# The model dimension of a mixture-of-experts trunk split as block and partition

## The chip, the core and the metric

The program runs on one core of a Trainium2 chip. A core has TensorE (PE; PEld are its weight loads), VectorE (DVE), ScalarE (ACT), GpSimd (POOL) and SyncE (SP), which here only issues transfers, and 16 DMA engines. The metric is the device time of one execution in microseconds (us), the median of several runs. All data is float32, and a matrix product of float32 shows as two instructions in the trace.

## What is computed

Two decoder layers over 256 tokens of 1024 values, each a token mixer and then a mixture of 32 experts of which a token uses two. Shifts, scales and gates of every sub-layer come from one conditioning vector.

```python
c_act = silu(c)
for i in range(2):
    sh_m, sc_m, g_m, sh_f, sc_f, g_f = split(c_act @ ada_w[i] + ada_b[i], 6)
    h = rmsnorm(x, norm_mix_g[i]) * (1 + sc_m) + sh_m
    y = pool_mixer(h, ...) if i == 0 else moba_attention(h, w_qkv, w_o)
    x = x + g_m * y
    h = rmsnorm(x, norm_ffn_g[i]) * (1 + sc_f) + sh_f
    # top-1 group of 8 experts, then top-2 experts in it
    for e in range(32):
        he = silu(h @ w_gate[e]) * (h @ w_up[e])      # 1024 -> 256
        y2 = y2 + combine[:, e] * (he @ w_down[e])    # 256 -> 1024
    x = x + g_f * y2
return rmsnorm(x, final_norm_g)
```

## The kernel before

The weights, some 270 MB, are read once each and in the order of use. They pass through `ring`, four slots of 24 KB a partition (3 MB each). SyncE's program is one list of transfers in that order. Before each load it waits on `ring_free` of the slot, which the engine that reads the slot's contents last has raised; a reader waits on `ring_full`. A slot holds one expert (gate, up and down, 1 MB each), or one of the sixteen pieces of `ada_w` (`ada`, 768 columns), or a quarter of `w_qkv`, or half of `w_o`. `split3` (line 299 on) cuts the last three into transfers of three, three and two blocks; each transfer raises `ring_full` by 16, and the reader waits for 48.

To contract over the 1024 values of the model dimension, they are cut into 8 blocks (k) of 128 partitions (p). The kernel before takes d = p*8 + k in all weights that are contracted over it but those of w_o and pool_w. So a partition's part of one expert's gate matrix is eight rows that lie next to each other in memory, 8 KB in one run. The activations have to be cut in the same way: the block k of a token's row is every eighth value. That is the view `h_str` in `gather` (the product that gathers each expert's tokens and turns them), `xr` in `transposes`, and `src` in `col_piece`, all of them stationary operands of TensorE with a step of 8 values (32 bytes).

The order of the work: three pieces of ada, the pooling mixer with ada pieces 3 to 7 around it, the router (`route`), the gather, 32 experts in a loop; then ada pieces 8 to 10, attention with 11 to 15 in its gaps, the router, gather and 32 experts of layer 1, and the last norm. An expert e on TensorE (`expert`): the products with gate and up from its gathered tokens `xe` (32 instructions), the four transposes of the result of expert e-1 (`turn_last`), the transpose of `he`, and down (8 instructions). GpSimd copies the tokens of the next expert into `xe`, ScalarE makes the silu and stores the turned result, and VectorE makes `he` (silu times up, line 1217), copies `heT` and `ye`, and raises `ring_free` for the slot. The experts are sorted by slot range, and after experts 20, 24 and 28 (`STAGES`) a quarter of the results is turned back and combined into the tokens (`combine`, TensorE with line 630 and 8 products), if all of its tokens are in.

Nine of the sixteen pieces of ada are multiplied by TensorE (`part`), seven by VectorE (`ada_steps(a, k0, k1)`: the steps k0 to k1 of piece a, one instruction for a block k of 768 columns). VectorE's program has the steps of piece 8 inside layer 0's last experts: steps 0 to 2 behind expert 30, ahead of expert 31.

The shifts and scales of three sub-layers are needed as columns, a value to a partition (`col`), because the activations are turned there. Each such set of 16 columns comes from three pieces of ada: 4, 5, 6 before layer 0's router, 8, 9, 10 between the layers, 12, 13, 14 within the attention. `col_piece` turns each column with a product of its own: the piece `acc` is stationary and a vector of ones is the moving side. In the attention ScalarE then copies them out (`take_columns`). `columns` adds the bias `bcol` and the norm's weight `gcol`, which SyncE loads with six small transfers, as it loads the router's weights into `stage_g` and `stage_e`.

Of the kernel before, what the change touches and what calls it, by code (L numbers as in the profile page):

```python
# [14 lines left out]
P = 128  # L15
# [3 lines left out]
T = SEQ // P  # L19
# [43 lines left out]

COL_OF = {4: 0, 5: 1, 6: 2, 8: 0, 9: 1, 10: 2, 12: 0, 13: 1, 14: 2}
# [37 lines left out]

def program(nc, x, c, ada_w, ada_b, norm_mix_g, norm_ffn_g, pool_w, pool_scale, w_qkv, w_o,
            router_group_w, router_expert_w, exp_w_gate, exp_w_up, exp_w_down, final_norm_g, misc, band, out):
    ctx = ExitStack()
    with ctx:
# [34 lines left out]
        h_str = reg_h[:, :].rearrange("p (t q k) -> p t k q", t=T, k=KC)  # L141
        bcol = sb("bcol", [P, 2, 2, KC])
# [28 lines left out]
        gcol = sb("gcol", [P, 3, KC])  # L171
# [76 lines left out]
        gate_d = exp_w_gate.rearrange("l e (p k) f -> l e p (k f)", k=KC)  # L248
        up_d = exp_w_up.rearrange("l e (p k) f -> l e p (k f)", k=KC)
        down_d = exp_w_down.rearrange("l e (j p) d -> l e p j d", p=P)  # L250
        ada_d = ada_w.rearrange("l (p k) n -> l p k n", k=KC)
        qkv_d = w_qkv.rearrange("l (p k) (g n) -> l p k g n", k=KC, g=3)
        bias_d = ada_b.rearrange("l (v p k) -> l v p k", v=6, k=KC)
# [44 lines left out]
        def _(sp):  # L298
# [12 lines left out]
            def qkv(j):  # L311
                split3(QKV_AT[j], qkv_w(QKV_AT[j][0]), qkv_d[0, :, :, :, j * 256:j * 256 + 256])
# [4 lines left out]
            def expert(L, e, s, freed):  # L317
                sp.wait_ge(S("ring_free", s), freed)
                gsrc, usrc, dsrc = gate_d[L], up_d[L], down_d[L]
                sp.dma_start(ring[:, s, 0:2048], gsrc[bass.ds(e, 1), :, :].rearrange("a p n -> (a p) n"))\  # L320
                    .then_inc(S("ring_full", s), 16)
                sp.dma_start(ring[:, s, 2048:4096], usrc[bass.ds(e, 1), :, :].rearrange("a p n -> (a p) n"))\
# [93 lines left out]
        def _(pe):  # L416
# [51 lines left out]
            def col_piece(a, dst):  # L468

                pe.wait_ge(*acc_done(a))  # L470
                one = quarter[:, 0:1] if a in ADA_PE else ones[:, 0:1]

                def turned(lo, hi, p0, which):
                    src = acc[:, a % 2, lo:hi].rearrange("p (q k) -> p k q", k=KC)
                    n = (hi - lo) // KC
                    for k in range(KC):
                        at = which * KC + k
                        last = mm(dst[p0:p0 + n, at:at + 1], src[:, k, :], one, True, True)
                    return last
# [404 lines left out]
        def _(act):  # L884
# [114 lines left out]
            def overflow(L):  # L999
                act.wait_ge(S("dn_free", L), E + 2)  # L1000
                n_ovf = act.value_load(ov_i[0:1, L, 2 * MAXOVF:2 * MAXOVF + 1], min_val=0, max_val=MAXOVF)
                with act.If(n_ovf > 0):
                    with act.Fori(0, n_ovf) as i:
# [3 lines left out]
                        act.dma_start(reg_h[:, :], gate_d[L][bass.ds(e, 1), :, :].rearrange("a p n -> (a p) n"))\  # L1007
# [199 lines left out]
        def _(dve):  # L1207
# [61 lines left out]
            def columns(i, src):  # L1269

                if i == 0:
                    dve.wait_ge(S("gcol_loaded"), 32)
# [328 lines left out]
```

## Time and profile before

| | us |
|---|---|
| Median of 3 runs | 881.61 (878.8 to 884.11) |
| The profiled execution, its own time | 879.25 |
| Its span, from the first to the last instruction | 877.5 |

The profile of one execution, busy time over the span:

| Engine | busy us | share |
|---|---|---|
| PE | 750.7 | 86% |
| PEld | 439.3 | 50% |
| DVE | 255.6 | 29% |
| ACT | 173.8 | 20% |
| POOL | 42.2 | 5% |

The rows of the trace that follow further down come from these views. The page cuts the span into 40 slices of 21.9 us and prints a value for each. The timeline lists instructions in order of time; in brackets stands how long the engine was idle before, and what ended that. Neighbours of one form are merged into one row, whose length is from the first start to the last end. The table of windows gives, for each stretch, the busy time of each engine with its instructions, the granted clock of TensorE as a share of 2.4 GHz, the mean busy share of the DMA engines (it can be a little over 1), and what they moved in GB/s. Layer 0's experts run from about 134 to 374 us, layer 1's from about 620 to 859.

### The profile page before, as it was taken

How to read it: one execution, taken by the hardware profiler on the slowest of the kernel's cores; microseconds unless marked ns; L12 is line 12 of the kernel's file. 1: busy time of each engine (PE TensorE's matmuls, PEld its weight loads, DVE VectorE, ACT ScalarE, POOL GpSimd, SP SyncE). 2: the span in 40 equal slices, each digit the busy share in tenths (PEclk: the TensorE clock that was granted, in tenths of full speed). 3: DMA queues.
4: the chain of work that ended last, by engine and by line, in shares of the span. 5: the costliest groups of instructions: out<-in, count | busy, mean ns of one | idle time of the engine just before them, and what ended most of it. 6: DMA issues, size and time to landing. Idle time of an engine off the chain costs nothing.

```text
span 877.5 us, 12384 instructions
## 1 busy us (share of the span) xinstructions
PE 750.7 (86%) x4574; PEld 439.3 (50%) x4574; DVE 255.6 (29%) x648; ACT 173.8 (20%) x394; POOL 42.2 (5%) x73
## 2 busy tenths in 40 slices
PE   3699778999988998957999979966899999898994
PEld 1265544444444444435878756444444444444441
DVE  0050371121112112267448333048111111211114
ACT  1322322111111111124123222142211111101112
POOL 0010001000000000000000000000100100000000
PEclk9898679999999999976999979967999999999998
DMA  9999715999999999998386452170399999999931
GB/s 342 398 379 410 308 77 184 420 415 417 417 418 418 418 417 416 400 360 328 144 288 233 151 223 91 70 288 0 147 408 418 418 419 418 418 416 416 417 128 49
DMA packets 71578, 274.25 MB, mean 313 GB/s; under 512 B 5727, under 2 KB 19295, under 8 KB 55022
## 3 DMA queue, kind: packets, MB, share of 16 engines
q1 hardware_dynamic: 71534, 273.64, 78.8%
q8 instruction: 30, 0.49, 0.2%
q14 instruction: 14, 0.11, 0.0%
HBM read 272.57 MB, written 1.05 MB: 312 GB/s over the span
## 4 chain that ended last, share of the span: by engine, by line
PE 74%; DVE 7%; DMA 7%; ACT 5%; issue 3%; SPq 2%; ACTq 1%; DVEq 0%; POOLq 0%; POOL 0%
PE bank L418 70%; DMA ring<-in_exp_w_down_dram 5%; DMA ring<-in_ada_w_dram 2%; DVE reg_c L1217 2%; PE bank L557 2%; DVE heT L1414 2%; ACT reg_c L969 2%; SPq L305 1%; ACT reg_b L886 1%; PE bank L630 1%; ACT reg_b L936 1%; ACTq L983 1%; DVE ye L1217 1%; PE bank L769 1%; ACT reg_h L905 1%
## 5 line engine op out<-in xcount | busy, mean ns | idle before, releaser
L418 PE MATMUL bank<-ring,xe 128*64 128x256 f32 x2048 | 232.6, 380 | 5.1 <-POOL xe L393 3.1
L418 PEld LDWEIGHTS bank<-ring,xe 128*64 128x64 f32 x2048 | 148.0, 137 | 106.5 <-issue 37.9
L418 PE MATMUL bank<-ring,heT 128*64 128x512 f32 x512 | 124.0, 605 | 24.6 <-DVE heT L1414 20.3
L969 ACT ACTIVATE reg_c<-bank 128x128 f32<-128x128 f32 x64 | 17.7, 277 | 366.0 <-PE bank L418 366.0
L1217 DVE TENSOR_TENSOR reg_c<-reg_c,bank 128x128 f32<-128x128 f32 x64 | 18.4, 287 | 236.9 <-ACT reg_c L969 236.9
L1417 DVE COPY ye<-bank 128x512 f32<-128x512 f32 x64 | 44.3, 692 | 138.4 <-PE bank L418 138.4
L393 POOL COPY xe<-reg_a 128x512 f32 x64 | 39.3, 614 | 754.6 <-PE bank L418 410.8
L418 PEld LDWEIGHTS bank<-ring,heT 128*64 128x64 f32 x512 | 31.1, 136 | 73.3 <-DVE heT L1414 36.8
L418 PE MATMUL bank<-reg_b,ring 128*128 128x256 f32 x256 | 63.2, 405 | 0.0
L418 PEld LDWEIGHTS bank<-reg_b,ring 128*128 128x128 f32 x256 | 51.3, 204 | 11.0 <-issue 2.7
L886 ACT ACTIVATE reg_b<-bank 128x512 f32 (+1 forms) x72 | 41.5, 576 | 54.2 <-PE bank L570 36.7
L418 PE MATMUL bank<-ring,cact 128*32 128x512 f32 (+1 forms) x288 | 34.3, 606 | 20.0 <-DMA rows<-in_final_norm_g_dram 14.3
L1220 DVE SCALAR_TENSOR_TENSOR acc<-ring,cact,acc 128x768 f32<-128x768 f32 x49 | 49.8, 1016 | 1.4
L570 PE MATMUL bank<-cst,ye 128*128 128x128 f32 x256 | 42.0, 286 | 1.8 <-DVE ye L1417 1.8
L418 PE MATMUL bank<-reg_b,reg_h 128*128 128x512 f32 x64 | 32.7, 675 | 11.6 <-DVE reg_b L1220 11.6
L570 PEld LDWEIGHTS bank<-cst,ye 128*128 128x128 f32 x256 | 26.8, 141 | 27.4 <-issue 23.9
L418 PE MATMUL bank<-ring,reg_a 128*128 128x512 f32 (+1 forms) x96 | 35.5, 524 | 0.6 <-ACT reg_b L886 0.6
L557 PE MATMUL bank<-cst,reg_c 128*128 128x128 f32 x64 | 21.0, 328 | 13.1 <-DVE reg_c L1217 13.1
L418 PEld LDWEIGHTS bank<-reg_b,reg_h 128*128 128x128 f32 x64 | 20.1, 317 | 23.1 <-issue 12.6
L418 PE MATMUL bank<-ring,reg_b 128*128 128x256 f32 x128 | 29.9, 386 | 0.0
L1220 DVE SCALAR_TENSOR_TENSOR reg_c<-cst,bank 128x384 f32<-128x384 f32 x16 | 9.7, 608 | 59.1 <-PE bank L418 59.1
L418 PEld LDWEIGHTS bank<-ring,reg_b 128*128 128x128 f32 x128 | 23.8, 191 | 5.9 <-ACT reg_b L886 1.3
(138 smaller groups left out, 564.3 us busy)
## 6 DMA issues: line engine op xcount, KB each, us to landing
ring<-in_exp_w_gate_dram SPq DMA_DIRECT2D x64, 1024.0 KB, 12.2
ring<-in_exp_w_up_dram SPq DMA_DIRECT2D x64, 1024.0 KB, 14.3
ring<-in_exp_w_down_dram SPq DMA_DIRECT2D x64, 1024.0 KB, 16.3
ring<-in_ada_w_dram SPq DMA_DIRECT2D x32, 1152.0 KB, 10.0
ring<-in_ada_w_dram SPq DMA_DIRECT2D x16, 768.0 KB, 12.7
ring<-in_w_qkv_dram SPq DMA_DIRECT2D x8, 1152.0 KB, 9.7
ring<-in_w_qkv_dram SPq DMA_DIRECT2D x4, 768.0 KB, 11.7
ring<-in_w_o_dram SPq DMA_DIRECT2D x4, 768.0 KB, 7.6
```

The source lines that it names most:

```text
L305: sp.dma_start(dst[:, a:b], src[:, a:b]).then_inc(S("ring_full", s), 16)
L393: nc.gpsimd.tensor_copy(xe[:, b, :, :], hS[:, :, bass.ds(off, CAP)]).then_inc(S("xe_ready", L), 1)
L418: return nc.tensor.matmul(o_, l_, r_, start=start, stop=stop)
L557: return nc.tensor.transpose(dst[:, 2 * P:3 * P], he[:, b, :], ident)
L570: last = nc.tensor.transpose(dst[:, cq * P:(cq + 1) * P], ye[:, b, cq * P:(cq + 1) * P], ident)
L630: last = nc.tensor.transpose(bank[half][:, mq * P:(mq + 1) * P], yT[:, half * 4 + mq, s * P:(s + 1) * P], ident)
L886: return nc.scalar.activation(o_, i_, ACT.Identity)
L969: nc.scalar.activation(sil[:, b, :], bank[b][:, 0:P], ACT.Silu).then_inc(S("sil_ready", L), 1)
L1217: return nc.vector.tensor_tensor(o_, a_, b_, op)
L1220: return nc.vector.scalar_tensor_tensor(o_, a_, s_, b_, op0, op1)
L1414: nc.vector.tensor_copy(heT[:, b, :], bank[b][:, 2 * P:3 * P]).then_inc(S("heT_ready", L), 1)
L1417: nc.vector.tensor_copy(ye[:, b, :], bank[2 + b][:, :]).then_inc(S("ye_ready", L), 1)
```

## The change

All weights contracted over the model dimension are read as d = k*128 + p, except `ada_w` and `c`. A gate or up matrix then goes to a partition in eight runs of 1 KB, 128 KB apart in memory. `h_str`, `xr` and `src` become blocks of 128 values side by side. `w_qkv` is fetched in three transfers by q, k and v in place of three by blocks; its runs are of 1 KB before and after. The router's weights come in runs of 16 bytes (group) and 128 bytes (expert), before of 128 bytes and 1 KB. `col_piece` turns 6, 6 and 4 blocks of 128 columns (16 products a set) in place of 8, 16 and 8 strided ones of 32 to 96 columns (32 products). Bias and norm weights of the columns are put in order on the host and come in one transfer `vecs`, which takes the place of six.

```diff
+COL_AT = (((8, 14),), ((14, 16), (0, 4)), ((4, 8),))
+COL_0, COL_N = (0, 6, 12), (6, 6, 4)
...
-        h_str = reg_h[:, :].rearrange("p (t q k) -> p t k q", t=T, k=KC)
-        bcol = sb("bcol", [P, 2, 2, KC])
+        h_str = reg_h[:, :].rearrange("p (t k q) -> p t k q", t=T, k=KC)
...
-        gate_d = exp_w_gate.rearrange("l e (p k) f -> l e p (k f)", k=KC)
-        up_d = exp_w_up.rearrange("l e (p k) f -> l e p (k f)", k=KC)
+        gate_d = exp_w_gate.rearrange("l e (k p) f -> l e p k f", k=KC)
+        up_d = exp_w_up.rearrange("l e (k p) f -> l e p k f", k=KC)
...
-        qkv_d = w_qkv.rearrange("l (p k) (g n) -> l p k g n", k=KC, g=3)
+        qkv_d = w_qkv.rearrange("l (k p) (g n) -> l p k g n", k=KC, g=3)
...
             def qkv(j):
-                split3(QKV_AT[j], qkv_w(QKV_AT[j][0]), qkv_d[0, :, :, :, j * 256:j * 256 + 256])
+                s, turn = QKV_AT[j]
+                sp.wait_ge(S("ring_free", s), turn)
+                for g in range(3):
+                    sp.dma_start(qkv_w(s)[:, :, g, :], qkv_d[0, :, :, g, j * 256:j * 256 + 256])\
+                        .then_inc(S("ring_full", s), 16)
...
-                sp.dma_start(ring[:, s, 0:2048], gsrc[bass.ds(e, 1), :, :].rearrange("a p n -> (a p) n"))\
+                sp.dma_start(gate_w(s), gsrc[bass.ds(e, 1), :, :, :].rearrange("a p k f -> (a p) k f"))\
...
-            sp.dma_start(gcol[:, 0:2, :], norm_ffn_g.rearrange("l (p k) -> p l k", k=KC)).then_inc(S("gcol_loaded"), 16)
-            sp.dma_start(gcol[:, 2, :], norm_mix_g[1].rearrange("(p k) -> p k", k=KC)).then_inc(S("gcol_loaded"), 16)
-            sp.dma_start(stage_g, router_group_w.rearrange("l (p k) n -> p l k n", k=KC)).then_inc(S("stage_loaded"), 16)
-            sp.dma_start(stage_e, router_expert_w.rearrange("l (p k) n -> p l k n", k=KC)).then_inc(S("stage_loaded"), 16)
-            for i, v0 in enumerate((0, 3)):
-                for which in range(2):
-                    sp.dma_start(bcol[:, i, which, :], bias_d[1, v0 + 1 - which]).then_inc(S("bcol_loaded"), 16)
+            sp.dma_start(vec[:, :], vecs).then_inc(S("vecs_loaded"), 16)
+            sp.dma_start(stage_g, router_group_w.rearrange("l (k p) n -> p l k n", k=KC)).then_inc(S("stage_loaded"), 16)
+            sp.dma_start(stage_e, router_expert_w.rearrange("l (k p) n -> p l k n", k=KC)).then_inc(S("stage_loaded"), 16)
...
-                if COL_OF[a] == 0:
-                    return turned(0, AC, 0, 1)
-                if COL_OF[a] == 1:
-                    turned(0, 256, 96, 1)
-                    return turned(256, AC, 0, 0)
-                return turned(0, 512, 64, 0)
+                for j in range(COL_N[COL_OF[a]]):
+                    at = (COL_0[COL_OF[a]] + j + KC) % (2 * KC)
+                    last = mm(dst[:, at:at + 1], acc[:, a % 2, j * P:(j + 1) * P], one, True, True)
+                return last
...
-                xr = h_of[i].rearrange("p t (q k) -> p t k q", k=KC)
+                xr = h_of[i].rearrange("p t (k q) -> p t k q", k=KC)
...
-                    dve.wait_ge(S("bcol_loaded"), 64)
                     then(tt(col[:, i, :, :], src, bcol[:, i - 1, :, :], ALU.add))
```

## Rows read from the trace of the kernel before

**Rows 1.** The page's line of what the DMA engines moved, 40 slices
```profile
GB/s 342 398 379 410 308 77 184 420 415 417 417 418 418 418 417 416 400 360 328 144 288 233 151 223 91 70 288 0 147 408 418 418 419 418 418 416 416 417 128 49
```
**Rows 2.** The page, the chain that ended last, shares of the span by line
```profile
PE bank L418 70%; DMA ring<-in_exp_w_down_dram 5%; DMA ring<-in_ada_w_dram 2%; DVE reg_c L1217 2%; PE bank L557 2%; DVE heT L1414 2%; ACT reg_c L969 2%; SPq L305 1%; ACT reg_b L886 1%; PE bank L630 1%; ACT reg_b L936 1%; ACTq L983 1%; DVE ye L1217 1%; PE bank L769 1%; ACT reg_h L905 1%
```
**Rows 3.** Timeline of PE, layer 0, two experts' gate and up: start us, us, engine line
```profile
175.11 3.62 PE L418 MATMUL bank<-ring,xe 128*64 128x256 f32 x32
...
181.98 3.62 PE L418 MATMUL bank<-ring,xe 128*64 128x256 f32 x32
```
**Rows 4.** Timeline of PE, layer 0, gate and up of experts 16, 20 and 31
```profile
244.05 3.67 PE L418 MATMUL bank<-ring,xe 128*64 128x256 f32 x32
...
274.37 3.67 PE L418 MATMUL bank<-ring,xe 128*64 128x256 f32 x32 [0.63 <-DMA ring<-in_exp_w_down_dram]
...
367.29 3.62 PE L418 MATMUL bank<-ring,xe 128*64 128x256 f32 x32
```
**Rows 5.** Timeline of PE, layer 1, gate and up of experts 20, 21 and 31
```profile
759.16 3.67 PE L418 MATMUL bank<-ring,xe 128*64 128x256 f32 x32
...
771.75 3.67 PE L418 MATMUL bank<-ring,xe 128*64 128x256 f32 x32
...
852.32 3.62 PE L418 MATMUL bank<-ring,xe 128*64 128x256 f32 x32
```
**Rows 6.** Timeline of PE, layer 1, a combine's eight unstrided products, 512 wide
```profile
768.15 3.67 PE L418 MATMUL bank<-mod,reg_c 128*128 128x512 f32 x8 [0.88 <-DVE mod L1440]
```
**Rows 7.** Windows while pool_w, w_qkv, w_o, ada_w and experts load, in this order
```profile
42.00:44.00 2.00, 2.00 (x8) 0.53 (x11) 0.95 (x2) 0.00 (x0) 0.00 (x0) 1.00 1.10 348
...
482.00:486.00 4.00, 4.00 (x23) 3.56 (x22) 0.00 (x0) 0.78 (x3) 0.00 (x0) 1.00 1.09 351
488.00:490.00 2.00, 2.00 (x13) 1.56 (x12) 0.00 (x0) 0.38 (x1) 0.00 (x0) 1.00 1.05 389
50.00:58.00 8.00, 8.00 (x34) 6.01 (x33) 0.37 (x1) 2.39 (x4) 0.00 (x0) 1.00 1.03 404
166.00:196.00 30.00, 27.35 (x193) 14.20 (x194) 5.36 (x13) 4.01 (x9) 2.84 (x5) 1.00 1.02 416
```
**Rows 8.** Timeline of DVE behind expert 30 of layer 0: piece 8, then expert 31's product
```profile
368.24 0.61 DVE L1238 TENSOR_SCALAR acc<-ring,cact 128x768 f32<-128x768 f32 x1
368.89 2.07 DVE L1220 SCALAR_TENSOR_TENSOR acc<-ring,cact,acc 128x768 f32<-128x768 f32 x2
371.34 0.29 DVE L1217 TENSOR_TENSOR reg_c<-reg_c,bank 128x128 f32<-128x128 f32 x1 [0.38 <-ACT reg_c L969]
```
**Rows 9.** Windows at the end of layer 0's experts (columns as in Rows 7)
```profile
376.00:380.00 4.00, 0.00 (x0) 0.00 (x0) 3.18 (x4) 0.60 (x1) 0.00 (x0) 0.97 1.04 388
380.00:384.00 4.00, 0.88 (x4) 0.88 (x5) 0.00 (x0) 0.00 (x0) 0.00 (x0) 0.50 1.09 349
```
**Rows 10.** Timeline of PE: column pieces 4, 5 with 6, 12, 13, 14; unstrided short products
```profile
75.72 3.04 PE L418 MATMUL bank<-cst,acc 128*96 128x1 f32 x16
...
83.72 4.62 PE L418 MATMUL bank<-cst,acc 128*32 128x1 f32 x48
...
106.21 0.53 PE L418 MATMUL bank<-ye,ones 128*128 128x32 f32 x4
...
107.02 0.39 PE L418 MATMUL bank<-ye,cst 128*128 128x32 f32 x2
...
453.57 2.93 PE L418 MATMUL bank<-ones,acc 128*96 128x1 f32 x16
...
473.91 3.15 PE L418 MATMUL bank<-ones,acc 128*32 128x1 f32 x32
...
489.21 2.08 PE L418 MATMUL bank<-ones,acc 128*64 128x1 f32 x16
```
**Rows 11.** Timelines of PE and PEld: eight transposes, then layer 1's gather weight loads
```profile
71.19 1.16 PE L503 MATMUL bank<-cst,reg_h 128*128 128x128 f32 x8 [0.80 <-ACT reg_h L905]
...
605.07 11.47 PEld L418 LDWEIGHTS bank<-reg_b,reg_h 128*128 128x128 f32 x27 [0.49 <-issue]
```

More of the change, by code:

```diff
@@ L100, in constants, with by_columns @@
     return {"misc": np.ascontiguousarray(misc), "band": band}
+def by_columns(ada_b, norm_mix_g, norm_ffn_g):
+    b = np.asarray(ada_b).reshape(2, 6, D)
+    rows = [norm_ffn_g[0], norm_ffn_g[1], norm_mix_g[1], b[1, 1], b[1, 0], b[1, 4], b[1, 3]]
+    return np.stack([np.asarray(r) for r in rows]).reshape(7, KC, P).transpose(2, 0, 1).reshape(P, 7 * KC)
 def program(nc, x, c, ada_w, ada_b, norm_mix_g, norm_ffn_g, pool_w, pool_scale, w_qkv, w_o,
-            router_group_w, router_expert_w, exp_w_gate, exp_w_up, exp_w_down, final_norm_g, misc, band, out):
+            router_group_w, router_expert_w, exp_w_gate, exp_w_up, exp_w_down, final_norm_g, vecs, misc, band, out):
     ctx = ExitStack()
@@ L170, in program @@
         spare = sb("spare", [P, 1])
-        gcol = sb("gcol", [P, 3, KC])
+        vec = sb("vec", [P, 7 * KC])
+        gcol = vec[:, 0:3 * KC].rearrange("p (i k) -> p i k", i=3)
+        bcol = vec[:, 3 * KC:7 * KC].rearrange("p (i w k) -> p i w k", i=2, w=2)
         col = sb("col", [P, 3, 2, KC])
@@ L319, in expert @@
                 gsrc, usrc, dsrc = gate_d[L], up_d[L], down_d[L]
-                sp.dma_start(ring[:, s, 0:2048], gsrc[bass.ds(e, 1), :, :].rearrange("a p n -> (a p) n"))\
+                sp.dma_start(gate_w(s), gsrc[bass.ds(e, 1), :, :, :].rearrange("a p k f -> (a p) k f"))\
                     .then_inc(S("ring_full", s), 16)
-                sp.dma_start(ring[:, s, 2048:4096], usrc[bass.ds(e, 1), :, :].rearrange("a p n -> (a p) n"))\
+                sp.dma_start(up_w(s), usrc[bass.ds(e, 1), :, :, :].rearrange("a p k f -> (a p) k f"))\
                     .then_inc(S("ring_full", s), 16)
@@ L471, in col_piece @@
                 one = quarter[:, 0:1] if a in ADA_PE else ones[:, 0:1]
[L473 to L479, printed above, removed]
-                if COL_OF[a] == 0:
-                    return turned(0, AC, 0, 1)
-                if COL_OF[a] == 1:
-                    turned(0, 256, 96, 1)
-                    return turned(256, AC, 0, 0)
-                return turned(0, 512, 64, 0)
+                for j in range(COL_N[COL_OF[a]]):
+                    at = (COL_0[COL_OF[a]] + j + KC) % (2 * KC)
+                    last = mm(dst[:, at:at + 1], acc[:, a % 2, j * P:(j + 1) * P], one, True, True)
+                return last
             def ada(a):
@@ L1103, in take_columns @@
             def take_columns(name, a):
-                src = unit(name)[:, 0:2 * KC].rearrange("p (w k) -> p w k", w=2)
-                if COL_OF[a] == 0:
-                    copy(craw[0:96, 1, :], src[0:96, 1, :]).then_inc(S("unit_read"), 1)
-                elif COL_OF[a] == 1:
-                    copy(craw[96:128, 1, :], src[96:128, 1, :])
-                    copy(craw[0:64, 0, :], src[0:64, 0, :]).then_inc(S("unit_read"), 1)
-                else:
-                    copy(craw[64:128, 0, :], src[64:128, 0, :]).then_inc(S("unit_read"), 1)
+                craw_f = craw[:, :, :].rearrange("p w k -> p (w k)")
+                src = unit(name)
+                for lo, hi in COL_AT[COL_OF[a]]:
+                    last = copy(craw_f[:, lo:hi], src[:, lo:hi])
+                last.then_inc(S("unit_read"), 1)
             def exps(m):
@@ L1271, in columns @@
                 if i == 0:
-                    dve.wait_ge(S("gcol_loaded"), 32)
+                    dve.wait_ge(S("vecs_loaded"), 16)
                 if i < 2:
@@ L1592 @@
     arrays, args = {}, {}
-    for name, a in [(n, inputs[n]) for n in _INS] + list(constants().items()):
+    vecs = by_columns(inputs["ada_b"], inputs["norm_mix_g"], inputs["norm_ffn_g"])
+    for name, a in [(n, inputs[n]) for n in _INS] + [("vecs", vecs)] + list(constants().items()):
         a = _np.ascontiguousarray(a)
```

7 lines of the change are left out of this document (4 added, 3 removed).

## The prediction

> **What bounds the kernel now.** I read the page's slices first: the transfer rate stands at 415 to 418 GB/s through most of layer 0's experts and again through layer 1's [rows 1]. The chain of what ended last gives TensorE's products 70% and the transfer of the expert's last matrix only 5% [rows 2]. The two do not contradict each other, and the timeline of TensorE shows why. One expert's gate and up matmuls start 6.87 us after those of the expert before (175.11 to 181.98) [rows 3]: that is TensorE's own pace. One expert's weights are 3 x 1.0486 MB, and at 416 to 418 GB/s they take over 7.5 us: the transfers are the slower of the two. The ring holds four experts, so TensorE starts each layer with a lead and loses it at 0.7 us per expert. In layer 0 it is used up at expert 16 (244.05); experts 16 to 20 start every (274.37 - 244.05) / 4 = 7.58 us, which I take as the period of the transfers [rows 4]. In layer 1 the lead ends at expert 20 (759.16) [rows 5]. The three combines in the last twelve experts then give TensorE extra work (771.75 - 759.16 = 12.59 us from one expert to the next, 5.7 more than 6.87), and the transfers get ahead again. So the loop is balanced to about 0.7 us per expert, and any slower transfer comes straight through.
>
> **Part 1, the expert weights in 1 KB runs.** Before, a gate or up matrix goes to a partition in one run of 8 KB; after, in eight of 1 KB. The trace of before holds 1 KB runs too, in w_qkv and pool_w, each in a stretch of its own, so their rate can be read alone. In the windows of the bulk transfers [rows 7] pool_w (1 KB rows that lie side by side in memory, as the new gate matrix's will) moves at 348 GB/s, w_qkv (1 KB rows far apart) at 351, w_o (2 KB) at 389, ada_w (3 KB) at 404, the experts' mix of 8 and 4 KB at 416. The share of the DMA engines is full in all five, so this is the rate of the run length and not a lack of work. I take 351, from the longer of the two 1 KB windows; 348 is the other end. One matrix then takes 1.0486 / 351 = 2.99 us in place of 1.0486 / 416 = 2.52, or 0.47 more; two of them 0.94; the period becomes 7.58 + 0.94 = 8.52 us (8.58 at 348 GB/s). With layer 0's first expert at 244.05 - 16 x 6.87 = 134.1 and layer 1's at 759.16 - 20 x 6.87 = 621.8, the lead is gone by the ninth expert in the one and the eleventh in the other.
>
> The Trainium skill (DMA: Bandwidth & Descriptors, Why small descriptors are slow) gives a packet a fixed 3 cycles beside one for each 32 bytes. By it a 1 KB run costs 35 cycles for 32, some 8% over an 8 KB run, and by that alone the period would be 8.0; the 348 and 351 GB/s of [rows 7] are 16% below 416, twice as much. Its Specifications table asks only 512 B for line rate, by which the change would cost nothing here; [rows 7] speak against that too.
>
> Layer 0: TensorE's expert 16 started when its weights had landed, so expert 4, the first loaded inside the loop, landed at 244.05 - 12 x 7.58 = 153.1. After: expert n lands at 153.1 + 0.94 + 8.52 (n - 4), so 28 at 358.5 and 31 at 384.1. Expert 28's combine lets 31 start at 358.5 + 12.59 + 2 x 6.87 = 384.8, against 367.29 now [rows 4].
>
> The wait behind it: VectorE's program has the first three steps of ada piece 8 between experts 30 and 31, now at 368.24 to 370.96, and expert 31's product only after them, at 371.34 [rows 8]. SyncE issues piece 8 behind expert 31, and with the queue full it lands 3.146 MB / 404 GB/s = 7.8 us after it, at 391.9. VectorE stands on that wait with expert 31's product queued behind, and TensorE, ScalarE and the tail wait for the product. It starts at 391.9 + 2.7 = 394.6, 23.2 us later than now; without this hold it would be 17.5. TensorE idles some 6 us for it. A like idle stretch now takes its clock from 0.97 to 0.50, the 1.2 GHz level [rows 9], so expert 31's down product (1.94 us) and what follows would run at half speed: +2.0 (0 to 4).
>
> Layer 1: 759.16 - 16 x 7.58 = 637.9 for expert 4; after, 28 lands at 637.9 + 0.94 + 24 x 8.52 = 843.3 and 31 starts at 843.3 + 12.59 + 13.74 = 869.6 against 852.32 [rows 5]: +17.3. Nothing but the tail follows.
>
> **Part 2, columns by whole blocks.** Each set of shift and scale columns took 64 TensorE instructions (32 products, two instructions each) with a stationary operand strided by 8; it takes 32 after, 128 wide and without stride. A contiguous load of 128 with a short product goes every (107.02 + 0.39 - 106.21) / 10 = 0.12 us, ten instructions in all [rows 10]. Before layer 0's router, 3.04 + 4.62 us [rows 10] become 12 x 0.12 + 20 x 0.12 to 0.24 (half clock is possible): a gain of 1.4 to 3.8, I take 2.8. In the attention, where TensorE is busy without a gap, 2.93 + 3.15 + 2.08 [rows 10] become 32 x 0.12 = 3.8; the gain is up to 4.3, and ScalarE's reads of the same banks may take some back: 3.8 (1 to 4.3). Between the layers piece 8's product is hidden, as TensorE then waits for piece 9 on VectorE; 0.3.
>
> **Part 3, gathers and transposes without stride.** The gather's weight loads are the longest of the kernel, but 27 of them start within 11.47 us, one per 0.425 us [rows 11], while the combine's eight products, as wide and without a stride, last 3.67 us, 0.46 each with their tail [rows 6]. The moving side paces both: no gain (0 to 1). Eight strided transposes take 1.16 us [rows 11]; a few hundredths each at most: 0.3 in all.
>
> **Part 4, small loads.** Six vector loads become one; the router weights come in 4096 runs of 16 and 128 B in place of 512 of 128 B and 1 KB. They may hold ada pieces 4 to 7 back by 1 to 3 us. Cover: those pieces are wanted from 65 us on, and the first experts not before 133. With it gone, up to 3. The wait for bcol goes; nothing was late on it. w_qkv keeps its 1 KB runs and only the grouping changes: 0.
>
> **The sum.** 23.2 + 2.0 + 17.3 - 2.8 - 3.8 - 0.3 - 0.3 = +35.3. On the profiled execution's 879.25 that is 914.6; the median shown, 881.61, is 2.4 above it and would give 916.9. I say 915. The bounds: rate +3.3, hold -5.7, clock -2 to +2, gains -2 to +4.5, small loads +3: 903 to 927. I widen it to 898 to 930, since the rate of 1 KB runs is read from windows of 2 and 4 us and must hold for 450.
>
> **Rivals.**
> - Half the price (7 in 100): next to each other in memory and with nothing mixed in, the new runs move like w_o's 2 KB rows, 389 GB/s. One matrix costs 2.70, the period is 7.94; both layers lose the 0.36 x 17 = 6.1 us up to expert 20, after which the combines give TensorE the lead back; the hold costs 1. 879.25 + 13.2 - 7.2 = 885. For it: the rate rises with the run. Against: pool_w lies side by side too, and gave 348. The 3-cycle rule of the Trainium skill, above, would land near here.
> - Faster (4 in 100): the new runs keep the full rate and parts 2 and 3 are left alone: 879.25 - 7.2 = 872. The point where it tips: 2 x 17 experts x the rise of the period = 7.2, a rise of 0.21, or a matrix in 2.62 us: 400 GB/s. 1 KB rows would have to beat the 3 KB rows' neighbourhood.
> - The clock (7 in 100): TensorE now waits 8.52 - 6.87 = 1.65 us in each of some 45 experts. If that lets its clock fall to the lower level in every third, that expert's 6.5 us of products double, of which 3.3 are won back in the next two: 15 x 3.2 = 48 at worst, about half that where the clock returns within the expert: 915 + 24 = 939. For it: [rows 9]. Against: there the idle stretch was over 7 us, and between 244 and 274 the waits of half a microsecond left the pace alone.
> - Otherwise 2 in 100; the forecast 80 in 100.
>
> **Chances.** A measurement of this kernel tells about 0.5% (4.4 us) from no change. Faster 0.04, the same 0.01, slower 0.95.
>
> **What would show it.** Rate in the expert stretches near 370 GB/s with the engines' share full (3.146 / 8.52 = 369); 128 matrices x 128 partitions x 7 = 115 thousand more packets; experts 8.5 us apart from the ninth on in layer 0 and the eleventh in layer 1, TensorE's waits put down to the weights' transfers; VectorE held before expert 31 of layer 0 by ada_w; column products halved in number and shorter; the gather as long as before. It would be wrong if the rate stays above 400, if the experts keep 6.87, or if the clock row drops inside the loops.

## The result and the profile after

The kernel after takes 907.95 us (median of 4 runs, 907.04 to 908.52) against 882.86 for the kernel before: ratio 1.029, 95% interval 1.024 to 1.034. That is slower by 25.1 us; the forecast was 915. The profiled execution has a span of 905.7 us against 877.5. The page of the kernel after, what the DMA engines moved and the chain of what ended last:

```profile
GB/s 346 381 357 384 366 21 346 369 365 367 369 363 367 367 364 369 378 388 373 226 279 272 100 232 139 103 176 1 331 368 363 369 368 363 369 365 365 369 266 47
...
PE 42%; SPq 40%; DVE 7%; DMA 5%; issue 3%; ACT 3%; POOLq 0%; DVEq 0%; POOL 0%; ACTq 0%
PE bank L427 39%; SPq L337 18%; SPq L335 16%; DMA ring<-in_ada_w_dram 4%; SPq L333 3%; SPq L314 2%; DVE acc L1218 2%; DMA ring<-in_exp_w_down_dram 1%; DVE reg_c L1215 1%; PE bank L556 1%; DVE x_sb L1215 1%; DVE heT L1411 1%; ACT reg_c L968 1%; PE bank L629 1%; DVE ye L1215 1%
```

Where 415 to 418 GB/s stood [rows 1], 363 to 369 stand in both layers' experts, and where TensorE's products were 70% of the chain [rows 2], SyncE's queue (SPq, the issues of gate, up and down) now has 40%. The DMA engines are full (windows of the kernel after, layer 0's and layer 1's experts; columns as in [rows 7], the last three are granted clock, share of the DMA engines, GB/s):

```profile
200.00:380.00 180.00, 148.87 (x993) 78.69 (x991) 28.09 (x65) 20.23 (x45) 12.28 (x20) 1.00 1.07 367
...
700.00:850.00 150.00, 122.38 (x822) 63.72 (x818) 23.55 (x55) 16.99 (x38) 11.02 (x18) 1.00 1.07 367
```

A rival is that SyncE itself is too slow, as it now issues 1024 runs for a matrix. Its timeline speaks against it (gate and up early in layer 0, then up and down in the transfer-bound stretch):

```profile
142.20 0.37 SPq L333 DMA_DIRECT2D ring<-in_exp_w_gate_dram  x1
142.66 0.53 SPq L335 DMA_DIRECT2D ring<-in_exp_w_up_dram  x1
...
251.74 4.57 SPq L335 DMA_DIRECT2D ring<-in_exp_w_up_dram  x1
256.40 3.40 SPq L337 DMA_DIRECT2D ring<-in_exp_w_down_dram  x1
```

The same 1024 runs are issued in half a microsecond early on and stand for 4.57 us later; down, whose runs did not change, stands for 3.40 us there and for 0.8 to 1.4 in the kernel before. So the issues are held up by what is in front of them, and SyncE's 40% of the chain are the transfers' time.

The timeline of TensorE of the kernel after: gate and up of layer 0's experts 8, 9 and 10; what lies behind expert 31; and the column pieces that answer to [rows 10].

```profile
183.01 3.62 PE L427 MATMUL bank<-ring,xe 128*64 128x256 f32 x32
...
191.04 3.67 PE L427 MATMUL bank<-ring,xe 128*64 128x256 f32 x32 [0.98 <-issue]
...
199.63 3.67 PE L427 MATMUL bank<-ring,xe 128*64 128x256 f32 x32 [1.51 <-issue]
...
380.41 3.62 PE L427 MATMUL bank<-ring,xe 128*64 128x256 f32 x32
...
390.43 0.47 PE L556 MATMUL bank<-cst,reg_c 128*128 128x128 f32 x1 [5.81 <-DVE reg_c L1215]
391.28 3.33 PE L427 MATMUL bank<-ring,heT 128*64 128x512 f32 x8 [0.38 <-DVE heT L1411]
...
397.37 1.85 PE L629 MATMUL bank<-cst,reg_b 128*128 128x128 f32 x8 [1.18 <-ACT reg_b L885]
```

```profile
76.22 1.50 PE L427 MATMUL bank<-cst,acc 128*128 128x1 f32 x12
...
81.09 2.39 PE L427 MATMUL bank<-cst,acc 128*128 128x1 f32 x20
...
467.62 1.40 PE L427 MATMUL bank<-ones,acc 128*128 128x1 f32 x12
```

Seen there: the ninth expert after the first is the first to wait; the period is (276.83 - 191.04) / 10 = 8.58 us. TensorE then stands 5.81 us ahead of expert 31's turned product. The column pieces take half of what they did.

Two rows of the kernel before were not among those of the prediction, and bear on it. The first is the unstrided ada product behind the first column set; the second answers to the last row of the first fence (timeline of TensorE of the kernel before, transposes of layer 0's last combine):

```profile
78.69 3.02 PE L418 MATMUL bank<-ring,cact 128*32 128x512 f32 x16
...
383.12 1.97 PE L630 MATMUL bank<-cst,reg_b 128*128 128x128 f32 x8 [7.21 <-issue]
```

In the second, TensorE waits 7.21 us for nothing that the profile shows; after, 1.18. The difference of the two timelines, step by step (us; each is a start in after minus the same start in before, less the steps above it):

| step | forecast | measured |
|---|---|---|
| to layer 0's expert 0 (133.84 to 128.01) | -3.1 | -5.8 |
| experts 0 to 31 (367.29 to 380.41, less the line above) | +17.5 | +19.0 |
| expert 31 to VectorE's product for it (371.34 to 390.09) | +5.7 | +5.6 |
| its down product at half clock, to the last turn | +2.0 | +1.5 |
| the unnamed wait ahead of the last combine | 0 | -6.0 |
| between the layers (412.01 to 425.76 at the q product) | -0.3 | -0.5 |
| attention (512.43 to 520.15) | -3.8 | -6.0 |
| to layer 1's expert 0 (619.51 to 627.11) | 0 | -0.1 |
| layer 1's experts (852.32 to 879.26) | +17.3 | +19.3 |
| the tail | 0 | +1.3 |
| sum (the terms are rounded) | +35.3 | +28.2 |

### The profile page after: what moved, and what is told of

It is laid out like the page before. It is cut to its first block, busy times and chain, and to the rows that moved or that the text cites. A ratio compares the mean times of both kernels' runs of the same rounds, so it can differ in the third digit from the quotient of the medians.

```text
span 905.7 us, 12185 instructions
## 1 busy us (share of the span) xinstructions
PE 744.1 (82%) x4478; PEld 425.1 (47%) x4478; DVE 255.8 (28%) x648; ACT 173.4 (19%) x394; POOL 40.5 (4%) x73
## 2 busy tenths in 40 slices
DMA packets 189001, 274.23 MB, mean 303 GB/s; under 512 B 8719, under 2 KB 153103, under 8 KB 188830
## 4 chain that ended last, share of the span: by engine, by line
PE 42%; SPq 40%; DVE 7%; DMA 5%; issue 3%; ACT 3%; POOLq 0%; DVEq 0%; POOL 0%; ACTq 0%
PE bank L427 39%; SPq L337 18%; SPq L335 16%; DMA ring<-in_ada_w_dram 4%; SPq L333 3%; SPq L314 2%; DVE acc L1218 2%; DMA ring<-in_exp_w_down_dram 1%; DVE reg_c L1215 1%; PE bank L556 1%; DVE x_sb L1215 1%; DVE heT L1411 1%; ACT reg_c L968 1%; PE bank L629 1%; DVE ye L1215 1%
## 5 line engine op out<-in xcount | busy, mean ns | idle before, releaser
L427 PEld LDWEIGHTS bank<-ring,xe 128*64 128x64 f32 x2048 | 150.4, 137 | 142.9 <-issue 51.0
L427 PEld LDWEIGHTS bank<-reg_b,reg_h 128*128 128x128 f32 x64 | 13.7, 217 | 28.9 <-issue 24.0
L1411 DVE COPY heT<-bank 128x128 f32<-128x128 f32 x64 | 18.7, 292 | 27.0 <-PE bank L556 27.0
```

The costliest lines, as they stand in the source:

```text
L427: return nc.tensor.matmul(o_, l_, r_, start=start, stop=stop)
L1411: nc.vector.tensor_copy(heT[:, b, :], bank[b][:, 2 * P:3 * P]).then_inc(S("heT_ready", L), 1)
```

## The experiments

Four questions: is it the length of a run that costs, and on which side; is the hold worth what it was priced at; what made the columns faster than forecast; and where did 6 us ahead of the last combine go. Times are medians; ratios are against the kernel before in the same session.

### The run length

**runs8, runs4, runs2**: the kernel after, with gate and up in runs of 8, 4 and 2 KB (the first line of the edit; the writes into the ring follow it). The experts' values are then not those of the reference; the amount of work is the same.

```diff
-        gate_d = exp_w_gate.rearrange("l e (k p) f -> l e p k f", k=KC)
+        gate_d = exp_w_gate.rearrange("l e (a p b) f -> l e p a (b f)", p=P, b=RUN)
```

> The kernel after, with gate and up matrices fetched in one run of 8 KB a partition as before; their rows then do not match the tokens' blocks, so the experts' values are other ones. Theory (the whole loss is the length of the runs, and all else in the change is gain): transfers back at 416 GB/s, experts paced by them 7.58 us apart and only from expert 16 on, no TensorE wait of 6 us before expert 31's product; the gains seen in after stay (5.8 us before layer 0's experts, 6.6 between the layers): about 865 us of span, 0.985 of before. Rival (the small loads, the grouping of w_qkv or the block layout itself cost something that the slow transfers cover): 870 us or more of span.

> The kernel after, with the gate and up matrices fetched in runs of 4 KB (d = a*512 + p*4 + b); everything else as after, so the gate and up products take other rows of h than the reference wants. Theory (rate follows the run length): down has had 4 KB runs all along; at 404 to 416 GB/s a matrix takes 2.52 to 2.60 us, the period is 7.56 to 7.72, and TensorE's lead lasts to expert 16 or further in both layers: 861 to 866, I say 862. If the cost is the number of pieces on the chip's side alone, 8 KB and 4 KB would be alike too: 861. Over 870 would say that the 8 KB run is worth more than its neighbours show.

> The kernel after, with the gate and up matrices fetched in runs of 2 KB (d = a*256 + p*2 + b) in place of 1 KB; everything else as after, so the gate and up products take other rows of h than the reference wants. Theory (the rate follows the run length; after's period of 8.58 us per expert leaves 8.58 - 2.52 = 6.06 us for two matrices, 346 GB/s): at the 389 GB/s that w_o's 2 KB runs had, a matrix takes 2.70 us, the period is 2.52 + 2 x 2.70 = 7.92 us. Layer 0's expert 31 starts about 27 x 0.66 = 18 us earlier than after's 380.4, but no earlier than TensorE's own pace allows (360.4 in runs8): 362 to 366; the same in layer 1. Time 873, range 866 to 880. Rival (the number of runs per issue, not their size, costs SyncE its time; 512 runs per matrix in place of 1024): the excess over 8 KB would be halved too, so it gives about the same here and isn't told apart by this run. Rival (only runs under 2 KB cost): 861.

Measured: 860.87 us (ratio 0.975, 0.970 to 0.980) with 8 KB, 864.76 (0.980, 0.973 to 0.987) with 4 KB, 876.7 (0.9955, 0.992 to 0.999) with 2 KB, against 907.95 with 1 KB. Windows inside layer 0's transfer-bound stretch, of the kernel with 4 KB and of the kernel with 2 KB:

```profile
243.00:267.00 24.00, 19.98 (x138) 10.83 (x140) 4.23 (x11) 3.23 (x7) 2.46 (x4) 1.00 1.03 410
```

```profile
200.00:272.00 72.00, 59.44 (x412) 31.57 (x410) 11.98 (x29) 8.75 (x20) 6.10 (x10) 1.00 1.04 394
```

The periods are 7.58 us at 8 KB (the kernel before, [rows 4], and runs8, (267.51 - 244.77) / 3), 7.68 at 4 KB ((266.93 - 243.89) / 3 in the timeline), 7.98 at 2 KB ((272.10 - 224.25) / 6) and 8.58 at 1 KB. The excess over 8 KB is 0.10, 0.40 and 1.00 us for 256, 768 and 1792 more runs per expert: it grows with their number, and on 16 engines is by our estimate 6 to 9 ns for each run. The whole loss of this change is in that factor: with 8 KB runs what is left of the change makes the kernel 2.5% faster. runs2 and runs4 lie in the ranges expected for them; runs8 has a span of 857.6 us, 7 under the 865 expected, as the expectation did not count that the 6.0 us ahead of the last combine are gone here too. So some 6 of its gain of 21 us belong to that wait (below).

**before_1k**: the kernel before, its 8 KB runs of memory kept, but each spread over the ring in 1 KB pieces (up likewise; TensorE's view of the slot follows).

```diff
-                sp.dma_start(ring[:, s, 0:2048], gsrc[bass.ds(e, 1), :, :].rearrange("a p n -> (a p) n"))\
+                both = ring[:, s, 0:4096].rearrange("p (k g f) -> p k g f", k=KC, g=2)
+                sp.dma_start(both[:, :, 0, :], gsrc[bass.ds(e, 1), :, :].rearrange("a p (k f) -> (a p) k f", k=KC))\
```

> The kernel before, with gate and up interleaved block by block in the ring, so that each of their transfers lands in eight pieces of 1 KB while the source stays one run of 8 KB a partition; nothing else changes. Theory (a transfer moves in pieces of 1 KB as soon as one side has them, and that alone costs): 367 GB/s and 8.58 us an expert as in after, time 881 + 19 + 19 + 1 = about 920 us, 1.045 of before. Rival (the cost comes from where the rows lie in memory, 128 KB apart): 416 GB/s, 7.58 us, time as before within 3 us.

Measured: 923.93 us (1.044, 1.038 to 1.050); window of layer 0's experts:

```profile
200.00:380.00 180.00, 147.55 (x975) 77.67 (x973) 28.27 (x66) 20.23 (x45) 12.94 (x21) 1.00 1.07 366
```

366 GB/s, as in the kernel after, though memory is read in the old order. In the kernel after it is the other way round: 1 KB rows in memory, 8 KB side by side in a partition of the ring. So it is not where the rows lie in memory: the smaller run of the two sides counts. By itself this part costs the kernel before 42 us, more than the 25 of the whole change.

### The hold

**no_hold**: the kernel after, VectorE's first three steps of ada piece 8 moved behind expert 31.

```diff
-                        if L == 0 and e + u == E - 2:
-                            ada_steps(8, 0, 3)
...
-                    ada_steps(8, 3, 7)
+                    ada_steps(8, 0, 7)
```

> The kernel after, with the first three steps of ada piece 8 moved from ahead of expert 31's product to behind it on VectorE. Theory A (the hold hides another wait: in before TensorE stood 6.5 us ahead of the last combine with nothing that the profile shows, in after it stood 6 us ahead of expert 31's transpose and then only 1.2 there): expert 31's product comes 6 us earlier, the wait ahead of the combine grows back to 7 us, and the time stays within 2 us of after's 908. Rival B (the hold costs what the prediction said, 5.7 us or more): about 902 us.

Measured: 903.24 us (1.023, 1.019 to 1.027), 4.7 under after. Timeline of TensorE, the last combine of layer 0:

```profile
389.31 1.15 PE L629 MATMUL bank<-cst,reg_b 128*128 128x128 f32 x8 [1.18 <-ACT reg_b L885]
...
395.01 5.46 PE L427 MATMUL bank<-reg_h,reg_c 128*128 128x512 f32 x6 [4.55 <-DVE reg_h L1437]
```

The transposes start 8.06 us earlier than in after (397.37), the product behind them only 5.30 (400.31): VectorE now has all seven steps of piece 8 ahead of the copy of reg_h, and TensorE waits 4.55 us for that. The time is that of rival B (about 902), so the hold and its price are shown; a step moved out of one queue position was again late at the next.

### Stride or number

**apart**: the kernel before, with ada pieces stored so that TensorE reads its columns without a stride (all but piece 14); still 32 products per set, 8 KB runs.

```diff
+            return acc[:, a % 2, 0:n].rearrange("p (k q) -> p k q", k=KC)
...
+                if split:
+                    dst = apart(a)
+                def block(k):
+                    return w[:, k, :].rearrange("p (q c) -> p c q", c=KC) if split else w[:, k, :]
```

> The kernel before, with 8 KB runs and the same 32 column products a set; only the pieces of ada that become columns are stored with the eight values of a partition apart, so that the stationary operands have no stride (all but piece 14). Theory (the stride is what makes the column products slow, some 1.9 ns a column): the sixteen 96-wide ones go from 2.9-3.0 us to about 1.8, the others a little shorter, TensorE's clock stays up behind them; 3 to 6 us less than before, 876 to 879 us. Rival (the number of products decides, stride or not): within 1.5 us of before.

**col_stride**: the kernel after, its products 128 wide and 16 to a set, but strided by 6 values; the columns then hold other values than the reference wants.

```diff
+                src = acc[:, a % 2, :].rearrange("p (q j) -> p j q", j=6)
-                    last = mm(dst[:, at:at + 1], acc[:, a % 2, j * P:(j + 1) * P], one, True, True)
+                    last = mm(dst[:, at:at + 1], src[:, j, :], one, True, True)
```

> The kernel after with its 16 column products per set kept in number (128 wide), but each stationary operand strided by 6 values in place of contiguous, so the columns hold other values than the reference wants. It tells the stride apart from the number of products: after's sets last 1.50 and 2.39 us before layer 0's router and 1.40, 1.40, 0.95 in the attention, before's 3.04, 4.62 and 2.93, 3.15, 2.08 with twice the number, 96 wide and strided by 8. Theory (the stride is what costs, as the kernel with de-interleaved pieces had 32 contiguous products in 1.52 and 2.59 us): the sets take 2 us or more where 1.50 stood and 3 or more where 2.39 stood, and the attention's 2 us or more where 1.40 stood; the whole kernel 3 to 8 us slower than after: 912. Rival (the number of products costs): no change, 908, the sets 1.50, 2.39, 1.40, 1.40, 0.95 as before. Also expected by the first: the granted clock in the windows behind the sets (80 to 85 us and 500 to 505 us) falls back from 0.85 and 1.00 to about 0.7 and 0.6, as in the kernel before.

Measured: apart takes 873.15 us (0.989, 0.985 to 0.993), 3 us under the expected range, and is faster than both kernels. Timeline of TensorE, its sets before layer 0's router, to be laid beside the 3.04 and 4.62 of [rows 10]:

```profile
75.94 1.52 PE L423 MATMUL bank<-cst,acc 128*96 128x1 f32 x16
77.39 1.92 PE L423 MATMUL bank<-ring,cact 128*32 128x512 f32 x16
...
80.83 2.59 PE L423 MATMUL bank<-cst,acc 128*32 128x1 f32 x48
```

And of the kernel col_stride, with half as many:

```profile
76.31 2.83 PE L427 MATMUL bank<-cst,acc 128*128 128x1 f32 x12
79.06 2.80 PE L427 MATMUL bank<-ring,cact 128*32 128x512 f32 x16
...
84.09 4.60 PE L427 MATMUL bank<-cst,acc 128*128 128x1 f32 x20
```

Nearly all of the gain is the stride's: without it, the full number of products is about as fast as half of them (1.52 and 2.59 against 1.50 and 2.39); with it, half of them take as long as the full number. The second line of each fence shows what was missed in the forecast: the ada product behind the set has no stride in any kernel and takes 2.80 us behind a strided set (3.02 in the kernel before) and 1.92 behind an unstrided one. The granted clock, third from the end, tells why (windows 79 to 82 us, just behind the first set, of before, col_stride, after and apart):

```profile
79.00:82.00 3.00, 3.00 (x24) 0.55 (x16) 0.00 (x0) 0.00 (x0) 0.00 (x0) 0.56 1.02 423
...
79.00:82.00 3.00, 3.00 (x21) 0.71 (x25) 0.00 (x0) 0.00 (x0) 0.00 (x0) 0.66 1.06 370
...
79.00:82.00 3.00, 3.00 (x48) 1.62 (x41) 0.00 (x0) 0.98 (x2) 0.00 (x0) 1.00 1.06 366
...
79.00:82.00 3.00, 3.00 (x62) 1.87 (x58) 0.00 (x0) 0.98 (x2) 0.00 (x0) 1.00 1.02 424
```

Behind the strided set the clock spends most of these 3 us at the 1.2 GHz level (0.50), and what follows pays; behind the unstrided one it does not. Further on the stride makes no such difference: between 88 and 90 us, behind the second set, the granted clock is 0.50 in all four. Layer 0's first expert starts at 134.34 us in col_stride, 133.84 in before, 128.01 in after and 127.64 in apart. The time of col_stride as a whole, 971.89 us (1.103, 1.095 to 1.110), can't be used: with other column values the router fills its experts otherwise and the overflow part runs (2352 packets of a second queue that no other run has). So of its expectation only the sets and the clock are tested, not the 912 us.

**gather_stride**: the kernel after, with the stationary operands of transposes and gathers strided by 8 values; h is then taken in another order than the weights want.

```diff
-        h_str = reg_h[:, :].rearrange("p (t k q) -> p t k q", t=T, k=KC)
+        h_str = reg_h[:, :].rearrange("p (t q k) -> p t k q", t=T, k=KC)
```

> The kernel after with the stationary operands of the transposes and of the gather strided by 8 values again, all else contiguous as after, so h is taken in another order than the weights want. Theory (the moving side paces the gather): the gathers last as long as after's 16.67 and 15.67 us within 0.3, the eight transposes 1.16 in place of 1.10, the whole within 1 us of after's: 908. Rival (the strided load paces where the clock is full): each gather 1 us longer or more, 910 or above. The mean of a weight load should rise from 217 to about 317 ns in both.

Measured: 907.59 us (1.028, 1.021 to 1.036), as after. Weight loads by form (count, busy us, mean ns), of after and of gather_stride:

```profile
L427 PEld LDWEIGHTS bank<-reg_b,reg_h 128*128 128x128 f32 x64 | 13.7, 217 | 28.9 <-issue 24.0 <-DVE reg_b L1218 4.8
```

```profile
L427 PEld LDWEIGHTS bank<-reg_b,reg_h 128*128 128x128 f32 x64 | 20.1, 317 | 22.5 <-issue 11.9 <-DVE reg_b L1218 4.8
```

A load takes 100 ns longer with the stride, and it costs nothing, as it lies beside a 512-wide product; layer 0's gather takes 16.56 us against 16.67.

### The wait ahead of the last combine

The kernels with the code of after had no such wait (after, no_hold, gather_stride and the three with longer runs), those with the code of before had it (before 7.21 us, apart 7.17, before_1k 6.93), with and without a hold. What sets the two groups apart is, among other things, where TensorE's instructions lie. At this place TensorE jumps over the overflow part. Its instructions come in packets of 16 KB. Taking 256 to a packet, as the section of the Trainium skill named below does, the jump goes in before from its instruction 3304 to about 3590, which is from block 12 into block 14; in after from 3240 to 3526, block 12 into 13. These numbers are an estimate from the program, no row of the trace shows them, and 3590 lies only 6 behind the start of block 14. The trace has this: in the kernel before, the DMA rows show one packet of instructions between 380 and 382 us, inside the wait, and none in the 25 us ahead of it. Two kernels move the code and nothing else, before_shift with the lines below in the kernel before, after_shift with 64 in place of 32 in the kernel after:

```diff
+            for _ in range(32):
+                pe.sem_inc(S("shift"), 1)
             for a in range(3):
                 ada(a)
```

> The kernel before with 32 increments of a semaphore that nobody reads ahead of TensorE's first product (it waits there for the first transfer anyway), so that all of TensorE's later instructions stand 32 places further on; nothing else. Instructions take 64 bytes and the trace fetches them in packets of 16 KB, so 256 to a block. At the end of layer 0 TensorE jumps over the overflow part: in the kernel before from instruction 3304 to about 3590, from block 12 into block 14; here from 3336 to 3622, from block 13 into block 14; in the kernel after from 3240 to 3526, block 12 into 13; in layer 1 always into the next block. Theory (the 7.2 us of issue wait ahead of the last combine of layer 0 is the fetch of a block that is not the next one): it goes, the transposes start about 1.2 us after ScalarE's copy, at 377 in place of 383.1. VectorE's products for ada piece 9 are next in line before the attention; they start as much earlier, so most of it reaches the end: 877 (875 to 880). Rival (the wait belongs to the semaphores or to the DMA's load at that place, which are the same here): the gap stays 7.2, 882.5.

> The kernel after with 64 such increments ahead of TensorE's first product, which puts the jump over layer 0's overflow part where it stands in the kernel before (from instruction 3304, block 12, into block 14). Theory of the code fetch: the wait of some 7 us comes back ahead of the transposes of the last combine of layer 0, which started at 397.37 with 1.18 of wait in after and would start at 403 to 404; VectorE's and TensorE's later work goes with it: 913 (910 to 915). Rival (that the hold on ada piece 8 takes the wait's place, or that it belongs to the transfers): as after, 908.

Measured: before_shift 872.01 us (0.990, 0.988 to 0.993), 3 under its expected range; after_shift 908.36 (1.033, 1.029 to 1.036), where 913 was expected and the rival said 908. The transposes, in before_shift:

```profile
378.23 1.97 PE L630 MATMUL bank<-cst,reg_b 128*128 128x128 f32 x8 [1.28 <-ACT reg_b L888]
```

and in after_shift, with the DMA rows of its window 394 to 396 us:

```profile
396.87 1.97 PE L629 MATMUL bank<-cst,reg_b 128*128 128x128 f32 x8 [1.96 <-issue]
```

```profile
q8 instruction: 1, 0.02, 3.5%
```

32 increments that nobody reads take the wait away and make the kernel before 1% faster; its span falls by 5.4 us. In before_shift a packet of instructions comes at 372.6 us, ahead of the jump, and none in the gap between turn and transposes. A second pair says the same: apart_part (below) waits 7.07 us, with a packet inside, and with the 32 increments (apart_shift) 1.29. That the wait is for a block of code fetched on demand is shown by these two pairs.

How long such a fetch takes is not shown, and here the expectation of after_shift failed: the packet comes right behind the jump, and the wait grows by 0.8 us, where the four kernels with the full wait lose some 6. In before the packet starts 5.3 us after expert 31's turn does (375.25 to 380.53), in after_shift 0.1 us after it (394.25 to 394.32). It is not the hold that covers it (before_1k has a hold of 5.85 us and the full wait). In those four, w_qkv was issued as 768 and 1152 KB transfers by then, in after_shift as 1024 KB ones; whether the fetch queues behind them was not tried. Nor is it shown why the median fell by 9.7 us where the span of the profiled execution fell by 5.4; the runs of before spread from 876.7 to 887.6 in that session, those of before_shift from 871.4 to 873.8, and the profiled execution of before_shift is the slowest of its six.

The Trainium skill (Runtime: NRT & Kernel Launch, Instruction fetch mechanics) says that fetching is sequential, in blocks of 256 instructions, and that a taken branch out of what is loaded has to fetch its target before it goes on. The trace agrees in that the packet falls into the wait; for the length of the wait no run here gives a rule.

### A better version

**apart_part** leaves pieces 8 and 9, which VectorE makes between the layers, as they were; **apart_shift** adds the 32 increments to it.

```diff
-                    if a == 14:
+                    if a in (8, 9, 14):
...
-                split = a in COL_OF and COL_OF[a] < 2
+                split = a in (12, 13)
```

> The kernel with de-interleaved ada pieces, but pieces 8 and 9, which VectorE makes between the layers, left as in the kernel before (VectorE writes them without a stride, TensorE reads them with one); pieces 4, 5, 6 and 10 (copied by ScalarE) and 12, 13 (VectorE, in the attention) stay de-interleaved. Theory: between the layers VectorE is the one waited for (7.33 us at 400.24 in the kernel with all of them, its six steps there 1.62 us each against 1.02), so the path to the attention gets 3.6 us back and loses about 1 on piece 9's products: 870.6 for the span becomes 868, the time 870.5 (868 to 873). If the strided steps of VectorE were hidden: 874 or more.

> The same as the kernel that leaves pieces 8 and 9 alone, plus the 32 increments ahead of TensorE's first product (jump at the end of layer 0 from instruction 3336 to 3622, block 13 into 14). Theory: both gains add, as they lie one behind the other: 870.5 - 5.5 = 865 (862 to 868), which would be the fastest correct kernel of this case, 2% under before. If VectorE's work between the layers doesn't start earlier with it, 870.

Measured: apart_part 874.83 us (0.993, 0.991 to 0.996): the expectation of 870.5 was wrong. The attention's q product does start 2.96 us earlier than in apart (407.61 against 410.57), as expected, but of this 1.66 us are left 80 us later, and 9 us further on apart_part is 0.7 behind. Timeline of TensorE behind piece 14's strided set, in apart and in apart_part:

```profile
487.16 0.87 PE L423 MATMUL bank<-ye,reg_b 128*64 128x256 f32 x8
487.96 0.93 PE L423 MATMUL bank<-reg_a 64*128 64x128 f32 x8
```

```profile
485.50 1.55 PE L423 MATMUL bank<-ye,reg_b 128*64 128x256 f32 x8
486.98 1.65 PE L423 MATMUL bank<-reg_a 64*128 64x128 f32 x8
```

The same program text there, the same strided set ahead, and the granted clock between 484 and 488 us is 1.00 in apart and 0.50 in apart_part. The eight products take 1.55 us in before, before_shift and apart_shift too, and 0.87 in before_1k; what decides it is not shown. apart_shift, with the wait gone as well, takes 868.30 us (865.32 to 871.25; 0.986, 0.983 to 0.989). That is at the upper end of what was expected (865, 862 to 868). It keeps the 8 KB runs, and is 13 us under before and some 40 under after; 10 of the 13 come with the increments alone (before_shift). apart with the increments, the next thing to try, was not run.

## Why the prediction was right, and where it was not

- **The rate.** Right in kind, a little off in size: period 8.52 forecast from w_qkv's 351 GB/s, 8.58 measured, which is what pool_w's 348 had given [rows 7]. Over both layers that makes +38.3 in place of 34.8. A few microseconds of a transfer read alone foretold 450 us of it to 1%.
- **The lead.** First waits at expert 9 of layer 0 and expert 10 of layer 1, ninth and eleventh forecast. The working took expert 31's landing as a fixed time, while the sum took the columns' gain off it as well. The runs bear the sum out: the loads start when TensorE frees their slots, so an earlier first expert makes them all earlier. By the sum expert 31 would start 14.4 us later than before, and it does 13.1. Layer 1's first expert, put at 621.8, stands at 619.51 in before: 2.0 us of other products lie behind expert 3, in both kernels, so this costs the forecast nothing.
- **The hold and the clock behind it.** 5.7 forecast, 5.6 in the trace, 4.7 by no_hold; half clock +2.0 forecast, +1.5 measured.
- **Columns.** The step that was mis-sized: 2.8 and 3.8 us forecast, 5.8 (with 0.3 of the transposes) and 6.0 measured. The sets alone gained 3.8 (7.66 to 3.89) and 4.4 (8.16 to 3.75), the upper ends of their ranges. The working priced the products alone and took the rows around them as they were; the 3.02 us product behind the set in before was itself slowed by it. The half-clock rows behind the sets were in the trace to be read.
- **Gathers, transposes, small loads.** No gain from the gathers, as forecast from the moving side. The router weights' 4096 short runs held nothing back that shows. Packets grew by 117 thousand (71578 to 189001), 115 forecast.
- **Not seen at all**: the 6.0 us of code fetch. The prediction cites the windows around it [rows 9] for the clock, and does not ask what TensorE waits for there. The change takes 64 instructions out ahead of the jump, and by the count above that moved its target into the next block. But with the jump back in its old place (after_shift) the wait is only 0.8 us longer, so of the 6.0 the place accounts for 0.8; the other 5.2, a fetch that is short in one kernel and long in the other, stay open. Against a kernel before without the wait (before_shift, another session) the change costs 36 us, not 25.
- **Rivals.** Half the price is ruled out by the period and by runs2, whose 7.98 and 876.7 are what 2 KB runs give. Full rate is ruled out by runs8 against after, 47 us apart. The clock in the loops stayed at 1.00 with a wait of 1.5 us in every expert. The Trainium skill's 3 cycles a packet (DMA: Bandwidth & Descriptors, Why small descriptors are slow) would by our estimate have given a period of 8.0; the measured excess is 1.0 us over 7.58, more than twice as much.

The three errors, -5.2 for columns (2.7 and 2.2, and 0.3 elsewhere), +3.5 for the rate and -6.0 for the fetch, with +1.3 for the tail and -0.6 for hold and clock, make the -7.1 between 35.3 and 28.2. That the total came so close is in part luck: the rate erred one way and two terms of 5 and 6 us the other. The bounds as listed reach from 905 to 927, not from 903.

## What to carry to other kernels

A loop that is balanced between an engine and its weights has no room for a slower transfer: before rearranging an axis so that an operand becomes contiguous, read the rate of that run length from a window where it moves alone, and count the shorter run of source and destination. A large share of the issuing engine in the chain, with the DMA engines' share at 1, is the transfers' own time. Take strides out of short products (one column wide) in the copy that writes the operand, where that engine is not the one waited for (VectorE's steps of 768 values took 1.62 us with a stride in apart, 1.02 without), and leave them in loads that lie beside a wide product. A wait of several microseconds put down to "issue" right behind a jump may be code: shift the program by a few instructions before explaining it otherwise, and be wary of ratios between programs of different length until then.

## What the runs showed of the hardware that was not expected

- 1, 2, 4 and 8 KB runs: 8.58, 7.98, 7.68 and 7.58 us for 3.146 MB, of which a third stays in 4 KB runs. The price grows with the number of runs, and 1 KB pieces on the chip's side alone (366 GB/s, before_1k) cost as much as 1 KB rows on the memory's side alone (367, after).
- Behind a jump, one packet of instructions fetched on demand cost some 6 us in four kernels and 0.8 in another; shifting the code by 32 instructions took it away in two.
- In the 3 us behind a strided set of short products the granted clock was 0.56 and 0.66, behind an unstrided one 1.00; behind the strided set of piece 14 it fell in some kernels and not in others.
- The issue of a transfer of 1024 runs took 0.37 to 0.53 us early in layer 0 and up to 4.57 where the DMA engines were full.
